# A fused chain of four mixer and feed-forward blocks on one NeuronCore: the opening re-ordered around the first modulation

## What is computed

```python
def rmsnorm(x, g):
    xf = x.astype(jnp.float32)
    y = xf * lax.rsqrt(jnp.mean(xf * xf, axis=-1, keepdims=True) + EPS)
    return (y * g.astype(jnp.float32)).astype(x.dtype)

def ada_modulate(x, c, norm_g, ada_w, ada_b):
    ada = jax.nn.silu(c) @ ada_w + ada_b
    shift, scale, gate = jnp.split(ada, 3, axis=-1)
    h = rmsnorm(x, norm_g) * (1.0 + scale[:, None, :]) + shift[:, None, :]
    return h, gate[:, None, :]

def even_layer(x, c, norm_g, ada_w, ada_b, in_w, pool_w, pool_scale, sgu_norm_g, sgu_w, sgu_b, out_w):
    h, gate_res = ada_modulate(x, c, norm_g, ada_w, ada_b)
    a, u, v, gate = _split(h @ in_w, EVEN_SIZES)
    ...
```

## Time and profile before

| | |
|---|---|
| median of 3 runs | 1046.85 us (1044.94 to 1047.94) |
| the profiled execution's own time | 1045.93 us |
| its span (first to last instruction) | 1044.2 us |
| TensorE busy | 1004.2 us, 96% of the span |
| VectorE, ScalarE, GpSimd busy | 723.6, 507.6, 41.7 us |
| DMA | 219.58 MB, mean 210 GB/s over the span |

### The profile page before, as it was taken

How to read it: one execution, slowest core, us unless ns; L and a number is a source line. 1 busy time by engine, 2 the same in 40 slices (tenths; PEclk the granted TensorE clock), 3 DMA queues, 4 the chain that set the end, 5 groups by cost and what they waited for, 6 DMA issues and landing times.

```text
span 1044.2 us, 19611 instructions
## 1 busy us (share of the span) xinstructions
PE 1004.2 (96%) x8234; PEld 991.3 (95%) x8234; DVE 723.6 (69%) x1027; ACT 507.6 (49%) x740; POOL 41.7 (4%) x69
## 2 busy tenths in 40 slices
PE   5999999999999999999999999999997999999998
PEld 5899999999999999999999999998997989999998
DVE  4867966777673856567889778667887665465554
ACT  2554354456524445634744464455556454444442
POOL 2100000000000003311000000000000000000000
PEclk9999999999999999999999999999999999999999
DMA  9987576657762884469467766755533446566621
GB/s 356 365 273 242 180 264 242 231 173 240 244 225 99 268 296 157 171 247 311 136 234 273 268 242 231 251 188 179 163 117 96 151 138 215 173 219 203 207 99 41
DMA packets 138960, 219.58 MB, mean 210 GB/s; under 512 B 7161, under 2 KB 110922, under 8 KB 138872
## 3 DMA queue, kind: packets, MB, share of 16 engines
q1 hardware_dynamic: 136776, 214.00, 59.5%
q10 hardware_dynamic: 1136, 2.58, 0.7%
q0 software_dynamic: 960, 1.76, 0.6%
HBM read 217.25 MB, written 1.05 MB: 209 GB/s over the span
## 4 chain that ended last, share of the span: by engine, by line
PE 84%; DVE 8%; ACT 3%; issue 2%; DMA 2%; SPq 1%; ACTq 0%; DVEq 0%
PE pw L550 62%; PE pacc L550 22%; DVE WL L1523 2%; DVE hl L1624 1%; DVE SQT L1619 1%; ACT AR L1083 1%; DMA ring<-in_even_in_w 1%; DVE ACC L1539 1%; DMA ring<-in_ada_w 1%; ACT hh L1083 0%; ACT WH L1083 0%; PE pw L930 0%; SPq L311 0%; DVE RS L1586 0%; ACT YH L1083 0%
## 5 line engine op out<-in xcount | busy, mean ns | idle before, releaser
L1083 ACT ACTIVATE WH<-ring 128x1024 fp32r<-128x1024 f32 x288 | 302.0, 1055 | 274.5 <-PE pw L550 194.5
L550 PE MATMUL pw<-hh,WH 128*128 128x256 f32 x1408 | 404.1, 287 | 8.8 <-DVE WL L1523 4.3
L1523 DVE TENSOR_TENSOR WL<-ring,WH 128x1024 fp32r<-128x1024 f32 x288 | 344.4, 1223 | 84.3 <-ACT WH L1083 83.8
L550 PE MATMUL pw<-hh,WL 128*128 128x256 f32 x1408 | 398.9, 283 | 0.0
L550 PE MATMUL pw<-hl,WH 128*128 128x256 f32 x1408 | 398.9, 283 | 0.0
L550 PEld LDWEIGHTS pw<-hh,WH 128*128 128x128 f32 x1408 | 270.6, 192 | 13.3 <-issue 10.2
L550 PEld LDWEIGHTS pw<-hl,WH 128*128 128x128 f32 x1408 | 270.7, 192 | 0.0
L550 PEld LDWEIGHTS pw<-hh,WL 128*128 128x128 f32 x1408 | 270.5, 192 | 0.0
L550 PE MATMUL pacc<-YH,WH 128*128 128x256 f32 x672 | 192.4, 286 | 3.5 <-issue 2.5
L550 PE MATMUL pacc<-YL,WH 128*128 128x256 f32 x672 | 190.8, 284 | 0.0
L550 PE MATMUL pacc<-YH,WL 128*128 128x256 f32 x672 | 190.8, 284 | 0.0
(11 more groups left out here) (245 smaller groups left out, 855.9 us busy)
## 6 DMA issues: line engine op xcount, KB each, us to landing
ring<-in_w_mod SPq DMA_DIRECT2D x72, 512.0 KB, 6.0
ring<-in_odd_in_w SPq DMA_DIRECT2D x56, 512.0 KB, 6.8
ring<-in_ada_w SPq DMA_DIRECT2D x48, 512.0 KB, 7.9
ring<-in_ffn_w_gate SPq DMA_DIRECT2D x44, 512.0 KB, 4.9
ring<-in_ffn_w_up SPq DMA_DIRECT2D x44, 512.0 KB, 5.2
ring<-in_ffn_w_down SPq DMA_DIRECT2D x44, 512.0 KB, 4.8
ring<-in_even_in_w SPq DMA_DIRECT2D x40, 512.0 KB, 6.9
ring<-in_even_out_w SPq DMA_DIRECT2D x16, 512.0 KB, 5.4
```

Of the source, the lines that this page charges most:

```text
L550: return eng.matmul(o, a, b, start=start, stop=stop, skip_group_check=True)
L1083: return eng.activation(dst, src, func, **kw)
L1523: tt(WL[:, i % NL, :], slot(half_of(i)), WH[:, i % NH, :].bitcast(F32), SUB).then_inc(s_lo, 1)
```

## The change

- **Units and order of halves.** The scale's chunk (`ada_w` columns 1024 to 2047) is loaded first, as halves 0 to 7; the shift's chunk is halves 8 to 15. In `MOD` and `ada_b` the places stay: chunk 0 of the sums now goes to `MOD[8:16]`, chunk 1 to `MOD[0:8]`.
- **Loads.** SP begins with the ring. The loads of c and cond are a pack of their own and come first in ACT's queue, ahead of the identity and x; the other seven small vectors and the rest of the constants are issued by ACT after the exponentials. POOL's sgu loads wait for half 19, not 15.
- **Who takes which half.** TensorE takes 1, 3, 6, 9, 12; VectorE takes 13, 14 and 15 last, and 11 after the first bias addition.
- **h by another way.** ACT multiplies x by r (`XR`, two activations of 128x1024), TensorE transposes that a second time (`xr0` to `xr3`, 16 transposes), ACT copies it to `SQT` (four of 128x512) and multiplies it in place by `GS` (eight of 128x256). `spread` and the eight L1619 instructions of VectorE are gone from the opening; `xT` is still made, for the residual.
- **The shift in two parts.** The sums of chunk 1 are closed after four column groups (`ada1a`) and after eight (`ada1`); VectorE adds the bias for each part; `hh` and `hl` of k = 0 to 3 follow the first, those of k = 4 to 7 the second. One ring piece is cut ahead of each part, where three (ACT) and two (DVE) were cut before all.
- `ACC2` lies in `AR`, since `SQT` is now written while chunk 1 is summed.

The diff, cut to its core:

```diff
-ADA_PE = (1, 3, 6, 11, 14)
+ADA_PE = (1, 3, 6, 9, 12)
...
-    units += ada(a0, 0, 2)
+    units += ada(a0, 1, 2) + ada(a0, 0, 1)
...
-    for key, ms in (("p0", (0, 2, 4)), ("p1", (5, 7, 8, 9, 10)), ("p2", (12, 13)), ("p3", (15,))):
+    for key, ms in (("p0", (0, 2, 4)), ("p1", (5, 7)), ("p2", (8, 10)), ("p3", (11,)), ("p4", (13, 14, 15))):
...
-        packs = [[("c", I["c"], 8), ("norm_g", I["norm_g"], 16), ("ada_b", I["ada_b"], 48),
+        packs = [[("c", I["c"], 8), ("cond", I["cond_2"], 8)],
+                 [("norm_g", I["norm_g"], 16), ("ada_b", I["ada_b"], 48),
...
 (TensorE)
+            ada_half(1)
+            ada_half(3)
             p.wait_ge(d_x, 16)
+            turn(XN, "xt")
...
+            close(last, "vc1")
+            ada_half(6)
+            p.wait_ge(s_xr, 2)
+            turn(XR, "xr")
+            p.wait_ge(*ada_done(7))
             p.wait_ge(d_cst, 16)
+            ada_sum(0, range(8), "ada0")
...
+            p.wait_ge(*gone["ada0"])
+            ada_half(9)
+            ada_half(12)
+            warm(8, "warm0a")
+            p.wait_ge(*ada_done(15))
+            ada_sum(1, range(4), "ada1a")
+            ada_sum(1, range(4, 8), "ada1")
+            warm(8, "warm0c")
...
 (ScalarE)
+            pack_loads(eng.dma_start, 0, d_vec[0])
             eng.dma_start(cst[:, 0:P], I["consts"][:, 0:P]).then_inc(d_id, 16)
             eng.dma_start(XN, I["x"].rearrange("o (a p) n -> p (o a) n", p=P)).then_inc(d_x, 16)
...
+            pack_loads(eng.dma_start, 1, d_vec[1])
+            eng.dma_start(cst[:, P:], I["consts"][:, P:]).then_inc(d_cst, 16)
...
+            s.wait_ge(s_r, 1)
+            for m in range(2):
+                act(XR[:, m, :], XN[:, m, :], scale=RS[:, m:m + 1]).then_inc(s_xr, 1)
+            for q in range(4):
+                evac(f"xr{q}", SQT[:, 2 * q:2 * q + 2, :], src=v3(pw[place[f"xr{q}"]][:, :], 2))
...
+            s.wait_ge(s_gs, 1)
+            for k in range(8):
+                s.wait_ge(*gone[f"xr{k // 2}"])
+                act(SQT[:, k, :], SQT[:, k, :], scale=GS[:, k:k + 1]).then_inc(s_u, 1)
...
-            cut(1 - AHEAD_L)
-            modulate(L_EVEN, M0[:, 0:8])
+            cut(-AHEAD_H)
+            s.wait_ge(s_mod, 2)
+            s.wait_ge(s_u, 8)
+            modulate(L_EVEN, M0[:, 0:8], range(4))
+            cut(1 - AHEAD_H)
+            s.wait_ge(*gone["ada1"])
+            modulate(L_EVEN, M0[:, 0:8], range(4, 8))
...
 (VectorE)
             ada("p2")
+            v.wait_ge(*gone["vc1"])
+            first_add(0, 8, 0, 8, "ada0")
...
+            ada("p3")
...
+            ada("p4")
+            first_add(1, 0, 0, 4, "ada1a")
+            cut(-AHEAD_L)
...
+            first_lows(range(4))
+            first_add(1, 4, 4, 4, "ada1")
             cut(1 - AHEAD_L)
+            v.wait_ge(*gone["ada1"])
+            first_lows(range(4, 8))
...
 (GpSimd)
-            g.wait_ge(*landed(15))
+            g.wait_ge(*landed(19))
...
 (SyncE)
-            pack_loads(eng.dma_start, 0, d_vec[0])
```

More of the change, by code:

```diff
@@ L339, in build @@
         d_id, d_cst, d_x = sem("d_id"), sem("d_cst"), sem("d_x")
-        d_vec = [sem(f"d_vec{a}") for a in range(3)]
-        n_vec = [16 * len(packs[0]), 16 * len(packs[1]), 16 * (len(packs[2]) + 1)]
+        d_vec = [sem(f"d_vec{a}") for a in range(4)]
+        n_vec = [16 * len(pk) for pk in packs[:3]] + [16 * (len(packs[3]) + 1)]
         d_sguw, d_sgub, d_glr, d_glw = sem("d_sguw"), sem("d_sgub"), sem("d_glr"), sem("d_glw")
@@ L351, in build @@
         s_silu = sem("s_silu")
+        s_xr = sem("s_xr")
+        s_gs = sem("s_gs")
         s_x2 = sem("s_x2")
@@ L509, in ysc @@
             return last
-        full, gone, place = {}, {"ada0": (s_mod, 1), "ada1": (s_mod, 2)}, {}
+        full, gone, place = {}, {"ada0": (s_mod, 1), "ada1": (s_mod, 3)}, {}
         block = ctx.enter_context(nc.Block())
@@ L689, in norm_mod @@
                 back(f"r{L}")
[L692 removed]
+            n0, n1, n2, n3 = pack_n
             def ada_half(m):
@@ L699, in ada_half, with ada_sum @@
                     last = mm(pacc[:, j, c * P:c * P + P], slot(g)[:, j * P:j * P + P],
-                              SIL[:, m % 8:m % 8 + 1].to_broadcast([P, P]), m in (1, 11) and j % 2 == 0, False)
+                              SIL[:, m % 8:m % 8 + 1].to_broadcast([P, P]), m == 1 and j % 2 == 0, False)
                 last.then_inc(s_adp, 1)
-            def ada_sum(c):
-                p.wait_ge(*ada_done(8 * c + 7))
-                for j in range(8):
+            def ada_sum(c, js, name):
+                for j in js:
                     last = mm(pacc[:, j, c * P:c * P + P], (ACC, ACC2)[c][:, j * P:j * P + P], ones, False, True)
-                close(last, f"ada{c}")
+                close(last, name)
             p.wait_ge(d_id, 16)
@@ L1120, in yhigh, with modulate @@
                 act(f2(YH[:, i % 3]), src).then_inc(s_yh, 1)
-            def modulate(L, sh):
-                for k in range(8):
+            def modulate(L, sh, ks=range(8)):
+                for k in ks:
                     s.wait_ge(s_u, 8 * L + k + 1)
@@ L1541, in ada @@
                     elif what == "add":
[L1542 to L1546 removed]
+                        v.wait_ge(*full[f"ada{c}"])
                         b = place[f"ada{c}"]
@@ L1635, in update, with first_add, first_lows @@
                 v.wait_ge(s_x, X_FIN[L] + 8)
-            n0, n1, n2 = pack_n
+            def first_add(c, to, j0, n, name):
+                v.wait_ge(*full[name])
+                tt(MOD[:, to:to + n].unsqueeze(2), pacc[:, j0:j0 + n, c * P:c * P + 1],
+                   col("ada_b", to, n).unsqueeze(2), ADD).then_inc(s_mod, 1)
+            def first_lows(ks):
+                for k in ks:
+                    v.wait_ge(s_hh, k + 1)
+                    stt(out=hl[:, k, :], in0=SQT[:, k, :], scalar=M0[:, k:k + 1], in1=hh[:, k, :].bitcast(F32),
+                        op0=ADD, op1=SUB).then_inc(s_hl, 1)
+            n0, n1, n2, n3 = pack_n
             v.wait_ge(*full["vc0"])
```

74 lines of the change are left out of this document (30 added, 44 removed).

## The result

| | before | changed |
|---|---|---|
| median of 8 executions each, taken together | 1047.46 us (1044.94 to 1048.77) | 1042.44 us (1041.82 to 1046.17) |
| the profiled execution's own time | 1045.93 us | 1042.68 us |
| its span | 1044.2 us | 1041.0 us |
| first large product / start of unit v1 | 37.01 / 43.54 us | 34.21 / 40.29 us |

The ratio of times is 0.9958, with a 95% interval of 0.9944 to 0.9972: 4.4 us less, 2.9 to 5.9. Two more sets of executions gave 0.9963 (0.9949 to 0.9977) and 0.9959 (0.9946 to 0.9973). The forecast was 1043.5 us, 3.4 us less, in a range of 1041.5 to 1046.3.

A forecast was written before the change was run, and what follows sets the result against it. TensorE, 96% busy, bounds it; only the opening can move. First addition 3.65 us earlier (0.77 landings, 2.9 order), then 0.2 longer: v1 3.4 earlier, 1045.93 to 1042.5 profiled; with 0.9 for the median, 1043.5 us, range 1041.5 to 1046.3.

The forecast's parts named there:

- The bound: Whole kernel: TensorE is busy 96% of the span, so time can change only in the opening, where it has nothing to do.
- Part 1, earlier landings: Opening loads: the ring's earlier start uses 314 KB of free DMA capacity, so half 15 lands 0.77 us earlier, at 28.84.
- Part 2, behind the last half: From half 15's landing to the shift's first addition: sums and addition no longer behind two low parts, 2.9 us won, ending 31.4.
- It keeps up: VectorE on halves 13 to 15: they land 1.3 us apart and cost 1.28 each, so half 15 is done at 30.14.
- Part 3, from addition to v1: From the shift's first addition to v1: steps sum to 8.67 us, 0.2 more than before, so v1 starts at 40.1.
- Part 4, the scale's way: Scale's sums before VectorE's last four halves: addition at 23.5 us, needed by 24.6, so hidden with 1.1 us of cover.
- The sign against it: VectorE's last halves: running 13 to 15 back to back with no DMA wait would show the scale's way was not hidden.
- Half clock: Rival, 12%: idle time in the new opening drops TensorE to half clock for 3.3 us, costing 1.6 us: 1045.1 us.
- The slower case: Rival, 5%: ten ring loads, 12.8 us of transfer, hold back c, the identity and x: 1047.5 to 1050 us.
- given back downstream: Rival, 5%: TensorE starts early and then waits for pieces 4 to 6: 1045 to 1046.5 us.
- The chances: Measured time against a 0.3% mark at 1043.7 us: faster by more 0.45, within 0.50, slower by more 0.05.

The follow-up runs named there:

- the delay of 2.42 us: Changed kernel with 12 warm matmuls ahead of the scale's sums and none ahead of the shift's sums; v1 at 41.01 us, 0.72 later.
- two variants: Changed kernel with 21 warm matmuls for 8 ahead of v0: ratio 0.9997 to the kernel before; changed kernel with h formed the old way: v1 at 43.84 us.

## Why the prediction was right, point by point

- **The bound** was right: only the opening moved, and all of it reached the end (1000.7 us behind v1 in both profiled executions, and 3.1 us between the times at one clock).
- **Part 1, earlier landings** was mis-sized. I took 0.77 us at half 15; 0.2 to 0.6 was measured at halves 13 and 16 without the other chip's executions, and v1 loses only 0.2 without it. The free capacity was there and was used, 354 GB/s between 2.5 and 3.75 us where the earlier trace rows has 213, and 403 from 5 to 8.75 where the kernel before has 355. By 27.5 us, summed over the windows, some 290 KB more had been moved than before, near the 314 KB that I had priced; at 408 GB/s that is 0.7 us. Why the landings show less of it was not settled.
- **Part 2, behind the last half** was right as a mechanism and 0.6 us off at the addition (31.82 + 0.16 = 31.98, not 31.4). Three sizes failed: the landing of half 13 by 0.2, the rate of VectorE by 0.2, and the sums with their hand-overs by 0.1. I took 1.28 us for each of three; in a row with a wait on the one before they come 1.39 apart, by the chain (26.50, 27.89, 29.28). "It keeps up" was wrong: from half 14 on VectorE is the later.
- **Part 3, from addition to v1** was right in its sum (8.31 us measured, 8.67 said): ACT's path with the table load, from 31.98 to the low part's end at about 40.14, is 8.2 us. TensorE's side was wrong: I had the first product at 33.2 and it came at 34.21. The step that failed left out the warm matmuls behind the sums, 1.95 us by the earlier trace rows's 1.95 for the same count. v0 then ends at 40.21, with the low part just there: the 0.9 us of idle time that I forecast does not exist. That the missing step did not move v1 was luck: its path came out as long as ACT's. The addition's 0.6 us too late and part 3's 0.4 too short also cancel in part, which leaves v1 at 40.29 against 40.1.
- **Part 4, the scale's way** was right. The addition came at 23.14 (said: 23.5), the transposes took 1.97 (said: 1.95), the cover was 1.7 us (said: 1.1), and the delay of 2.42 us cost 0.72. The sign against it did not come: halves 13 to 15 ran back to back, but behind a wait of 1.71 us for half 13's landing.
- **The rivals.** Half clock did not come in the opening of the changed kernel's three profiled executions, but it did in two variants, for some 3.4 us by their windows, when TensorE idled 2.2 us ahead of the shift's sums. The slower case needs c behind the ring: the first transpose, which needs c and the identity, came at 7.37 us, earlier than the 9.14 of the earlier trace rows, so it was far off. Of the rule that each DMA engine takes turns between its queues, the trace shows this much: the identity landed 5.6 us after its issue and x about 10 us, with SP issuing its ten ring loads, 12.8 us of transfer, at the same time. They were slowed and not stopped. That agrees with the page of the Trainium skill ("DMA: Bandwidth & Descriptors", "Queues, rings and completion order"). Nothing was given back downstream: the 144 products behind v1 run without a step of another engine, as before.
- **The chances.** 0.45 for a gain above 0.3%, which is what was measured, 0.42% by the ratio; at one clock it is 3.1 us, just at that line, so the side on which it fell hangs on the clock. The forecast for the profiled execution, 1042.5, met 1042.68; the medians differ by more, and part of that is the clock, which the forecast treated as equal.

## What to carry to other kernels

Where an engine's list has slow work that waits for data in front of short work that others wait for, swapping the two is not enough if the same engine also has the work behind it: here the order alone gave 0.5 us, and with the new order kept, eight products put back on VectorE cost 3.2. A load stream that is already full gains what capacity was free, not what issue time is saved, and even that may not reach the last landing. Count warm-up work as work: 1.95 us of it stood in front of the first product and held it back by 0.55, unseen in the waits. And compare landings and times on one chip and at one clock: on the other chip a landing came 0.35 us later here, as much as the whole of part 1.

## What the runs showed of the hardware

- A chain of VectorE instructions that each wait for the one before takes 1.39 us a piece where one is 1.28: 0.11 us of hand-over for each.
- In three kernels with the same loads TensorE idled 2.2 us ahead of the shift's sums, behind 2 us of warm matmuls. One kept full clock (that of the 23.26 us row above, idle from 28.77 to 30.99 us), the other two fell to half, for some 3.4 us. Idle time of this length makes a fall possible and not certain. At a later layer start with 1.77 us of idle time a fall cost 1.3 us of the span, and over an execution 0.001 of mean clock goes with 0.6 to 0.65 us, which is most of the scatter of the times.
- A load of 64 KB that landed 1.9 us after its issue in the kernel before took 5.6 with the ring's loads on the way (4.8 and 5.0 in two other executions of the changed kernel), and x of 1 MB took 10 instead of 5.6, with no loss here.
- With the issue of a full stream of 512 KB loads moved 3.3 us earlier, the fifth load landed 2.1 us earlier and the seventeenth 0.3.
- One kernel, profiled once on each of two chips, had half 13 at 26.53 and 26.88 us and half 16 at 30.62 and 31.09. The kernel before took 0.8 us more on the second chip at the same mean clock.
